# The first weight transfer of a convolution layer split into one contraction block each, the second half queued behind x's first block

## The chip, the cores and the metric

The kernel runs on one core of a Trainium2 chip. The metric is device microseconds (us) of one execution; each run gives one time, and the runs of a kernel are told by their median.

## The reference, cut to what matters

One layer of a convolution module over 1024 rows and 1024 channels, all in float32:

```
hn   = rms_norm(x) * norm_g                 # x: 1024 x 1024
a, b, gate = split(hn @ w_in, 3)            # w_in: 1024 x 3072
u    = a * sigmoid(b)
u    = depthwise causal conv of 31 taps over the rows + conv_b
u    = silu(layer_norm(u)) * silu(gate)
y    = x + u @ w_out                        # w_out: 1024 x 1024
```

## The kernel before, in words

Every float32 operand of a matmul is held as a high part, rounded to the matmul type (`w_hi`, `x_hi`), and a low part, the rest (`w_lo`, `x_lo`). One product is three matmuls: high by high, low weight by high x, high weight by low x. ScalarE (ACT) makes the high parts by a copy with rounding, VectorE (DVE) or GpSimd (POOL) the low parts by a subtraction.

The input projection is cut into 24 units, a unit being 128 output channels. A unit takes the contraction over 1024 channels in eight blocks of 128 (k = 0 to 7), for each half h of the rows (512 columns of a matmul). All of the kernel's matmuls stand in one order on TensorE (PE), written out by hand. What follows concerns its head:

- TensorE first does 11 warm-up matmuls on a tile of ones (L756; the float32 type makes 22 instructions of them), which need nothing but that tile.
- Then come the first two units ("b" and "a" of channel block 0) on half 1, interleaved (`project_raw(1)`, `raw_term`, L651): for each k the three terms of both units, so six matmuls a block and 48 in all. x isn't normalized yet; the factor 1/rms is put on afterwards. A matmul waits on the count `w_first_hi` or `w_first_lo` of converted weight pieces and on the count of converted x blocks.
- The same two units follow on half 0. After its block k = 4, TensorE spreads the inverse rms of half 1 over the partitions with two matmuls (`spread_rms(1)`, L622 and L624). L622 needs the four high diagonals that VectorE makes from the inverse rms (L1082), L624 the four low ones (L1085).
- All other units (`project`, L634) and, after them, the output products (L710) follow.

SyncE (SP) issues the loads, all on one DMA queue, in an order written out by hand. For half 1: weight piece 0, x blocks 0 and 1, piece 1, x blocks 2 and 3, piece 2, x blocks 4 and 5, piece 3, x blocks 6 and 7 (`load_first_weights` L522, `load_columns` L499). A weight piece holds two contraction blocks of both units, 256 KB, 2 KB per partition; an x block is 256 KB as well. The identity, half 0's x blocks and rows 4 to 7 of x (512 KB each, `load_rows`, L495) come next, mixed; row tile 7 is queued just ahead of x block 4 of half 0. The third unit's weights (L504) and the taps wait on SP until the pieces that cover k < 4 are converted (L534).

ScalarE converts in the same order: piece 0 (`split_first`, L784), x block 0 (`split_raw`, L778), x block 1, piece 1, and so on; then half 0's x blocks, with a sum of squares of a row tile (L772) behind each of the first four. VectorE follows it with the low parts (L1107 and L1100); on half 0 it makes diagonals 4 and 5 before x block 4's low part, and 6 and 7 before block 5's (`DIAGS_BEFORE`, L74). GpSimd makes the inverse rms of each row tile (L1408, L1411), and the low part of the third unit's weights (L1424) once all of x's low parts are there.

`FIRST_PIECES` (L96) and `PIECE_BEFORE` (L97) say how many pieces there are and ahead of which x block each one is loaded and converted.

Of the kernel before, what the change touches and what calls it, by code (L numbers as in the profile page):

```python
# [11 lines left out]
P = 128  # L12
HALF = 512
# [19 lines left out]
for n in range(14 - POOL_TAPS):  # L33
# [57 lines left out]
         for part in (("22", "12") if (b, q) == (5, 3) else ADDS[b])]  # L91
# [1 line left out]
EARLIER_ADD = {(b, part, q): max([n for b2, part2, q2 in POSTS if (part2, q2) == (part, min(q, 3))  # L93
                                  for n in [POST[b2, part2, q2]] if n < POST[b, part, q]], default=None)
               for b, part, q in POSTS}
FIRST_PIECES = 4  # L96
PIECE_BEFORE = {0: 0, 2: 1, 4: 2, 6: 3}  # L97
WARM_UPS = 11


def gated_conv_layer(nc, x, x_t, w_first, w_in, w_out, per_channel, identity, out):
    T, D = x.shape
    NT, KC = T // P, D // P
# [29 lines left out]
    with ctx:  # L133
        def sb(name, shape, dt=F32, into=ctx):
            return into.enter_context(nc.sbuf_tensor(name, shape, dt))

        def sem(name):
            return ctx.enter_context(nc.semaphore(name))
# [6 lines left out]
        raw = sb("raw", [P, 2, KC * P])  # L145
# [63 lines left out]
        rms_ready = sem("rms_ready")  # L209
        w2lo_half_ready = sem("w2lo_half_ready")  # L210
        norm_in = sem("norm_in")
        w_first_in = [sem(f"w_first_in{i}") for i in range(FIRST_PIECES)]
        w_first_hi = sem("w_first_hi")
        w_first_lo = sem("w_first_lo")
        xhi_raw = sem("xhi_raw")
# [156 lines left out]
        def bank(job):  # L372
            return mm[:, BANK[job], :]
# [23 lines left out]
        def col_order(h, k):  # L397

            return KC * (1 - h) + k
# [8 lines left out]

        def first_raw(i):

            return raw[:].rearrange("p m c -> p (m c)")[:, HALF * i:HALF * (i + 1)]

        def first_raw_units(i):

            return first_raw(i).rearrange("p (m c) -> p m c", m=2)

        def first_units(w, i):

            ks = KC // FIRST_PIECES
            return w[:, 0:2, ks * i:ks * (i + 1), :].rearrange("p m k n -> p m (k n)")  # L420

        def nth(kind, m):

# [35 lines left out]
        def terms(hi1, lo1, hi2, lo2):  # L459
            return ((hi1, hi2), (hi1, lo2), (lo1, hi2))  # L460

        def half(h):
            return slice(h * HALF, (h + 1) * HALF)
# [28 lines left out]
        def _(sp):  # L492
            def load_rows(t):

                sp.dma_start(sgate[:, t, :], x[t * P:(t + 1) * P, :]).then_inc(x_sq_in[t], 16)  # L495

            def load_columns(h, k):

                sp.dma_start(nat[:, k, half(h)], x_t[h, k]).then_inc(xt_in[h][k], 16)  # L499

            def load_weights(m):

                kind, j = UNITS[m]
                sp.dma_start(raw[:, m % 2, :], w_in[PART[kind], j]).then_inc(raw_in[m % 2], 16)  # L504
# [14 lines left out]

            def load_first_weights(i):  # L520

                sp.dma_start(first_raw(i), w_first[i]).then_inc(w_first_in[i], 16)  # L522

            for k in range(KC):
                if k in PIECE_BEFORE:
                    load_first_weights(PIECE_BEFORE[k])
                load_columns(1, k)
            sp.dma_start(ident[:], identity).then_inc(ident_in, 16)
            for k in range(KC):
                for t in ROWS_BEFORE.get(k, ()):  # L530
                    load_rows(t)
                load_columns(0, k)
                if k == 5:
                    sp.wait_ge(w_first_lo, FIRST_PIECES // 2)  # L534
                    load_weights(2)
                    sp.dma_start(chan[:, KC:], per_channel[:, KC:]).then_inc(chan_in, 16)
            for t in range(TPH):
                load_rows(t)
                if t == 2:
                    sp.wait_ge(w_first_lo, FIRST_PIECES)  # L540
                    load_weights(3)
            for m in range(4, NU):
                if m == 5:
# [71 lines left out]
        def _(pe):  # L615
# [22 lines left out]

            def raw_term(m, h, k, i):

                piece = k // (KC // FIRST_PIECES) + 1
                if i == 0:
                    if h == 1:
                        pe.wait_ge(w_first_hi, piece)
                    pe.wait_ge(xhi_raw, col_order(h, k) + 1)
                elif i == 1:
                    pe.wait_ge(xlo_raw, col_order(h, k) + 1)
                elif h == 1:
                    pe.wait_ge(w_first_lo, piece)
                w, xx = terms(w_hi, w_lo, x_hi, x_lo)[i]  # L650
                return nc.tensor.matmul(bank(("unit", m, h)), w[:, m, k, :], xx[:, k, half(h)],  # L651
                                        start=(k == 0 and i == 0), stop=(k == KC - 1 and i == 1))

            def project_raw(h):

                for k in range(KC):
                    for i in (0, 2, 1):
                        for m in range(2):
                            ins = raw_term(m, h, k, i)
                            if (k, i) == (KC - 1, 1):  # L660
                                ins.then_inc(unit_ready[UNITS[m][0]], 1)
                    if (h, k) == SPREAD_AT[1]:
                        spread_rms(1)
# [102 lines left out]
        def _(act):  # L766
# [8 lines left out]
            def split_raw(h, k):  # L775

                act.wait_ge(xt_in[h][k], 16)
                nc.scalar.activation(x_hi[:, k, half(h)], nat[:, k, half(h)], ACT.Copy,  # L778
                                     scale=norm_g[:, k:k + 1]).then_inc(xhi_raw, 1)

            def split_first(i):

                act.wait_ge(w_first_in[i], 16)
                nc.scalar.activation(first_units(w_hi, i), first_raw_units(i), ACT.Copy).then_inc(w_first_hi, 1)  # L784
# [169 lines left out]
            for k in range(KC):  # L954
                if k > 0 and k in PIECE_BEFORE:
                    split_first(PIECE_BEFORE[k])
                split_raw(1, k)
# [110 lines left out]
        def _(dve):  # L1068
# [28 lines left out]
            def split_raw(h, k):  # L1097

                dve.wait_ge(xhi_raw, col_order(h, k) + 1)
                nc.vector.scalar_tensor_tensor(x_lo[:, k, half(h)], nat[:, k, half(h)], norm_g[:, k:k + 1],  # L1100
                                               x_hi[:, k, half(h)].bitcast(F32), ALU.mult,
                                               ALU.subtract).then_inc(xlo_raw, 1)

            def split_first(i):

                dve.wait_ge(w_first_hi, i + 1)
                nc.vector.tensor_tensor(first_units(w_lo, i), first_raw_units(i), first_units(w_hi, i).bitcast(F32),  # L1107
                                        ALU.subtract).then_inc(w_first_lo, 1)
# [23 lines left out]
            def conv_in(m, h):  # L1132

                _, j = UNITS[m]
                dve.wait_ge(unit_ready["a"], arrival(j, h))
                if (j, h) in RAW_ORDER:
                    dve.wait_ge(sig_scaled, 3 * RAW_ORDER.index((j, h)) + 3)
                else:
                    dve.wait_ge(sig_ready, arrival(j, h) - len(RAW_ORDER))
                if j >= 4:  # L1140
                    if j - 4 in STEP_END:
                        dve.wait_ge(steps_done, STEP[j - 4, "sum", HT - 1])
                    else:
                        dve.wait_ge(prod_ready, PRODUCT_END[j - 4])
                nc.vector.tensor_tensor(u[:, j % 4, 0:2, PAD + h * Q:PAD + (h + 1) * Q],
                                        bank(("unit", m, h)).rearrange("p (s q) -> p s q", q=Q),
                                        sig[:, h, :].rearrange("p (s q) -> p s q", q=Q), ALU.mult).then_inc(u_ready, 1)
# [128 lines left out]
            for k in range(KC):  # L1276
                if k > 0 and k in PIECE_BEFORE:
                    split_first(PIECE_BEFORE[k])
                split_raw(1, k)
# [298 lines left out]
```

## Time and profile before

| | |
|---|---|
| median of 3 runs | 354.58 us (354.42 to 354.72) |
| the profiled execution | 354.64 us, of which 352.8 us are its span |
| TensorE busy | 348.5 us, 99% of the span |
| VectorE, GpSimd, ScalarE busy | 91%, 76%, 66% |
| DMA | 43.51 MB, mean 123 GB/s; 9 tenths or more of the 16 engines' time in nearly all of the first 28 us |

The span runs from the first instruction to the last; the profiled execution's time is 1.8 us more, work around the program. All times below are from the span's start. The busy shares say which engine has room left over the whole span, not what a stretch waits for; for that the chain of waits and the timeline of the stretch are read. TensorE's weight loads (PEld) run beside its matmuls (PE), and the ends of matmuls are modelled, so starts are read rather than ends.

### The profile page before, as it was taken

How to read it: one execution, taken by the hardware profiler on the slowest of the kernel's cores; microseconds unless marked ns; L12 is line 12 of the kernel's file. 1: busy time of each engine (PE TensorE's matmuls, PEld its weight loads, DVE VectorE, ACT ScalarE, POOL GpSimd, SP SyncE). 2: the span in 40 equal slices, each digit the busy share in tenths (PEclk: the TensorE clock that was granted, in tenths of full speed). 3: DMA queues.
4: the chain of work that ended last, by engine and by line, in shares of the span. 5: the costliest groups of instructions: out<-in, count | busy, mean ns of one | idle time of the engine just before them, and what ended most of it. 6: DMA issues, size and time to landing. Idle time of an engine off the chain costs nothing.

```text
span 352.8 us, 4758 instructions
## 1 busy us (share of the span) xinstructions
PE 348.5 (99%) x1564; PEld 289.6 (82%) x1564; DVE 322.4 (91%) x516; ACT 232.0 (66%) x334; POOL 267.0 (76%) x192
## 2 busy tenths in 40 slices
PE   8999999999999999999999999999999999999996
PEld 8888888888888888888888888888888888878785
DVE  5679799999999999989999998998599999999972
ACT  6889685667936870998669777975784872443400
POOL 0119999999999999789999999895596551359240
PEclk9999999999999999999999999999999999999999
DMA  8995111201410321404110410441643498047152
GB/s 265 411 412 212 39 59 59 88 34 61 118 61 16 88 78 59 119 2 119 59 60 3 119 59 15 107 119 61 215 143 120 130 394 313 0 151 224 45 208 90
DMA packets 30520, 43.51 MB, mean 123 GB/s; under 512 B 18336, under 2 KB 18848, under 8 KB 30496
## 3 DMA queue, kind: packets, MB, share of 16 engines
q1 hardware_dynamic: 30352, 43.21, 36.5%
q8 instruction: 12, 0.20, 0.2%
q14 instruction: 12, 0.10, 0.1%
q10 hardware_dynamic: 144, 0.00, 0.0%
HBM read 34.82 MB, written 4.19 MB: 111 GB/s over the span
## 4 chain that ended last, share of the span: by engine, by line
PE 92%; DVE 5%; issue 1%; ACT 0%; DVEq 0%; ACTq 0%
PE mm L634 68%; PE acc L710 9%; PE mm L651 6%; PE mm L710 6%; DVE sgate L1254 2%; DVE nat L1266 2%; DVE x_lo L1234 1%; PE acc L756 1%; PE acc L691 1%; PE acc L701 1%; PE acc L628 0%; ACT x_hi L948 0%; PE acc L622 0%; PE acc L624 0%; DVE ones L1069 0%
## 5 line engine op out<-in xcount | busy, mean ns | idle before, releaser
L634 PE MATMUL mm<-x_hi,w_hi 128*128 128x512 f32 x352 | 137.4, 390 | 0.0
L634 PE MATMUL mm<-x_hi,w_lo 128*128 128x512 f32 x352 | 137.0, 389 | 0.0
L634 PE MATMUL mm<-x_lo,w_hi 128*128 128x512 f32 x352 | 137.0, 389 | 0.0
L1178 DVE SCALAR_TENSOR_TENSOR acc<-u,chan,acc 128x512 f32<-128x512 f32 x157 | 110.5, 748 | 0.1
L1484 POOL TENSOR_TENSOR pconv<-pconv,prod 128x512 f32<-128x512 f32 x60 | 78.4, 1349 | 1.3 <-ACT prod L865 1.3
L634 PEld LDWEIGHTS mm<-x_hi,w_lo 128*128 128x128 f32 x352 | 66.1, 188 | 13.8
L634 PEld LDWEIGHTS mm<-x_lo,w_hi 128*128 128x128 f32 x352 | 66.1, 188 | 13.6
L634 PEld LDWEIGHTS mm<-x_hi,w_hi 128*128 128x128 f32 x352 | 66.1, 188 | 13.4
L1178 DVE SCALAR_TENSOR_TENSOR acc<-u,w_sum,acc 128x512 f32<-128x512 f32 x90 | 67.2, 747 | 2.5 <-ACT acc L847 2.3
L865 ACT ACTIVATE prod<-u,chan 128x512 f32<-128x512 f32 x69 | 47.9, 716 | 19.9 <-POOL pconv L1484 18.5
L1428 POOL TENSOR_TENSOR w_lo<-raw,w_hi 128x1024 fp32r<-128x1024 f32 (+1 forms) x21 | 50.3, 2395 | 8.7 <-ACT w_hi L814 8.6
L1484 POOL TENSOR_TENSOR pool_before<-pool_before,prod 128x512 f32<-128x512 f32 x37 | 49.3, 1331 | 1.1
L1444 POOL TENSOR_TENSOR wb_lo<-raw,wb_hi 128x1024 fp32r<-128x1024 f32 x6 | 14.5, 2408 | 16.2 <-DVE x_lo L1234 10.8
L865 ACT ACTIVATE prod<-u,w_sum 128x512 f32<-128x512 f32 x30 | 21.5, 716 | 7.8 <-POOL pool_before L1484 7.4
L948 ACT ACTIVATE x_hi<-sgate 128x512 fp32r<-128x512 f32 x28 | 15.9, 625 | 16.0 <-DVE sgate L1254 16.0
L710 PE MATMUL acc<-wb_hi,x_hi 128*128 128x512 f32 (+1 forms) x68 | 25.8, 379 | 0.0
L710 PE MATMUL acc<-wb_lo,x_hi 128*128 128x512 f32 (+1 forms) x68 | 25.6, 377 | 0.0
L710 PE MATMUL acc<-wb_hi,x_lo 128*128 128x512 f32 (+1 forms) x68 | 25.6, 377 | 0.0
L814 ACT ACTIVATE w_hi<-raw 128x1024 fp32r<-128x1024 f32 x22 | 23.1, 1048 | 1.3 <-PE mm L634 0.9
L891 ACT ACTIVATE sgate<-nat 128x1024 uint16<-128x1024 uint16 x14 | 14.0, 1050 | 11.5 <-POOL nat L1475 8.9
L1234 DVE TENSOR_TENSOR x_lo<-sgate,x_hi 128x512 fp32r<-128x512 f32 x28 | 20.8, 801 | 0.0
L904 ACT ACTIVATE rows<-sgate 128x1024 uint16<-128x1024 uint16 x14 | 18.2, 1368 | 3.5 <-DMA sgate<-sgate 2.1
(109 smaller groups left out, 527.6 us busy)
## 6 DMA issues: line engine op xcount, KB each, us to landing
raw<-w_in SPq DMA_DIRECT2D x22, 512.0 KB, 3.3
nat<-x_t SPq DMA_DIRECT2D x16, 256.0 KB, 5.4
sgate<-x SPq DMA_DIRECT2D x8, 512.0 KB, 10.2
raw<-w_out SPq DMA_DIRECT2D x8, 512.0 KB, 3.3
nat<-x SPq DMA_DIRECT2D x8, 512.0 KB, 7.7
y<-nat SPq DMA_DIRECT2D x15, 256.0 KB, 2.2
raw_late<-w_out SPq DMA_DIRECT2D x4, 512.0 KB, 4.3
sig<-w_out SPq DMA_DIRECT2D x4, 512.0 KB, 4.1
```

Of the source, the lines that this page charges most:

```text
L634: ins = nc.tensor.matmul(bank(("unit", m, h)), w[:, m % 3, k, :], xx[:, k, half(h)], start=(k == 0 and i == 0), stop=(k == KC - 1 and i == 2))
L651: return nc.tensor.matmul(bank(("unit", m, h)), w[:, m, k, :], xx[:, k, half(h)], start=(k == 0 and i == 0), stop=(k == KC - 1 and i == 1))
L710: ins = nc.tensor.matmul(product_bank(b, q), v[:, k0 + k, rows], w[:, k, piece_columns(b, q)], start=(k == 0 and i == 0 and continued(b, q ...
L814: nc.scalar.activation(w_hi[:, m % 3, :, :].rearrange("p k n -> p (k n)"), raw[:, m % 2, :], ACT.Copy).then_inc(whi_ready, 1)
L865: nc.scalar.activation(dst, chain_in(j, chain, k), ACT.Identity, scale=tap(j, chain, k), bias=bias(j, chain) if k == 0 else 0.0).then_inc( ...
L904: nc.scalar.activation(words_of_rows(side)[:, :, :, i], crossed()[:, NT * i:NT * (i + 1), :], ACT.Copy).then_inc(rows_joined, 1)
L948: nc.scalar.activation(v_pair(b, k)[0], v_raw(b, k), ACT.Copy).then_inc(vhi_ready, 1)
L1178: ins = nc.vector.scalar_tensor_tensor(dst, chain_in(j, chain, k), tap(j, chain, k), chain_bank(j, chain), ALU.mult, ALU.add)
L1234: nc.vector.tensor_tensor(lo, v_raw(b, k), hi.bitcast(F32), ALU.subtract).then_inc(vlo_ready, 1)
L1428: nc.gpsimd.tensor_tensor(w_lo[:, m % 3, ks, :].rearrange("p k n -> p (k n)"), raw[:, m % 2, ks.start * P:], w_hi[:, m % 3, ks, :].rearran ...
L1444: ins = nc.gpsimd.tensor_tensor(lo, source, hi.bitcast(F32), ALU.subtract)
L1484: ins = nc.gpsimd.tensor_tensor(pool_sum(chain), summand, prod[:, SLOTTED.index((j, chain, k)) % 4, :], ALU.add)
```

## The change

Piece 0, which held contraction blocks 0 and 1 of both units, becomes two pieces of one block each; the other three pieces stay. The first (128 KB) is still the first load; the second (128 KB) is loaded and converted behind x's first block and ahead of its second. Since a partition of a piece now has to be laid out block by block, the host stores the pieces with the block outermost (block, unit, column), and the conversions read and write three-dimensional patterns (unit, block, column), where they had runs of 256. The two new loads read 1 KB per partition. TensorE's counts, and SP's two waits, follow the new number of pieces (SP waits for 3 pieces where it waited for 2, and for 5 where it waited for 4); the warm-ups stay 11.

```diff
-FIRST_PIECES = 4
-PIECE_BEFORE = {0: 0, 2: 1, 4: 2, 6: 3}
+FIRST_PIECES = ((0, 1), (1, 2), (2, 4), (4, 6), (6, 8))
+PIECE_BEFORE = {ks[0]: i for i, ks in enumerate(FIRST_PIECES)}
 WARM_UPS = 11
...
-        w_first_in = [sem(f"w_first_in{i}") for i in range(FIRST_PIECES)]
+        w_first_in = [sem(f"w_first_in{i}") for i in range(len(FIRST_PIECES))]
...
         def first_raw(i):
 
-            return raw[:].rearrange("p m c -> p (m c)")[:, HALF * i:HALF * (i + 1)]
+            k0, k1 = FIRST_PIECES[i]
+            return raw[:].rearrange("p m c -> p (m c)")[:, 2 * P * k0:2 * P * k1]
 
         def first_raw_units(i):
 
-            return first_raw(i).rearrange("p (m c) -> p m c", m=2)
+            return first_raw(i).rearrange("p (k m n) -> p m k n", m=2, n=P)
 
         def first_units(w, i):
 
-            ks = KC // FIRST_PIECES
-            return w[:, 0:2, ks * i:ks * (i + 1), :].rearrange("p m k n -> p m (k n)")
+            k0, k1 = FIRST_PIECES[i]
+            return w[:, 0:2, k0:k1, :]
...
             def load_first_weights(i):
 
-                sp.dma_start(first_raw(i), w_first[i]).then_inc(w_first_in[i], 16)
+                k0, k1 = FIRST_PIECES[i]
+                start = 2 * P * (k0 % 2)
+                sp.dma_start(first_raw(i), w_first[k0 // 2, :, start:start + 2 * P * (k1 - k0)]).then_inc(w_first_in[i], 16)
...
                 if k == 5:
-                    sp.wait_ge(w_first_lo, FIRST_PIECES // 2)
+                    sp.wait_ge(w_first_lo, PIECE_BEFORE[KC // 2])
...
                 if t == 2:
-                    sp.wait_ge(w_first_lo, FIRST_PIECES)
+                    sp.wait_ge(w_first_lo, len(FIRST_PIECES))
...
             def raw_term(m, h, k, i):
 
-                piece = k // (KC // FIRST_PIECES) + 1
+                piece = sum(ks[0] <= k for ks in FIRST_PIECES)
...
-    w_first = w_in[[1, 0], 0].reshape(2, P, KC // 2, 2 * P).transpose(2, 1, 0, 3).reshape(KC // 2, P, HALF)
+    w_first = w_in[[1, 0], 0].reshape(2, P, KC // 2, 2, P).transpose(2, 1, 3, 0, 4).reshape(KC // 2, P, HALF)
```

## Rows read from the trace of the kernel before

**Rows 1.** The page: TensorE's busy time, and its granted clock in 40 slices.

```profile
PE 348.5 (99%) x1564; PEld 289.6 (82%) x1564; DVE 322.4 (91%) x516; ACT 232.0 (66%) x334; POOL 267.0 (76%) x192
...
PEclk9999999999999999999999999999999999999999
```

**Rows 2.** The chain of waits in order of time: start us, us, what; the first 25 us.

```profile
1.03 5.07 PE acc L756 x22
6.10 17.92 PE mm L651 x78
...
24.25 0.23 PE acc L624
```

**Rows 3.** All waits of TensorE in the whole span: total us, times, longest us.

```profile
PE acc L756 <- DVE ones L1069: 1.0, 1, 1.0
PE mm L710 <- DVE x_lo L1234: 0.5, 1, 0.5
```

**Rows 4.** Weight loads of warm-ups and first units: ns min/median/max, first and last start us.

```profile
L756 PEld LDWEIGHTS acc<-ones x22: 288/333/338, 1.0 to 5.5; 128*128 128x128 f32 x22
...
L651 PEld LDWEIGHTS mm<-x_hi,w_hi x32: 187/188/333, 5.7 to 27.0; 128*128 128x128 f32 x32
```

**Rows 5.** Timeline, 0 to 12 us: start us, us, instruction [idle before <-releaser].

```profile
0.72 0.39 SPq L522 DMA_DIRECT2D raw<-w_first  x1
...
1.17 0.89 SPq L499 DMA_DIRECT2D nat<-x_t  x2
...
3.36 0.63 ACT L784 ACTIVATE w_hi<-raw 128x512 fp32r<-128x512 f32 x1 [0.71 <-DMA raw<-w_first]
...
4.16 0.72 ACT L778 ACTIVATE x_hi<-nat,chan 128x512 fp32r<-128x512 f32 x1 [0.17 <-DMA nat<-x_t]
...
6.48 0.63 ACT L784 ACTIVATE w_hi<-raw 128x512 fp32r<-128x512 f32 x1 [0.73 <-DMA raw<-w_first]
...
7.54 0.61 PE L651 MATMUL mm<-x_hi,w_hi 128*128 128x512 f32 x2
...
8.90 0.61 PE L651 MATMUL mm<-x_hi,w_hi 128*128 128x512 f32 x2
```

**Rows 6.** Stretches: us, each engine's busy time, PEclk, DMA share, GB/s.

```profile
4.00:5.00 1.00, 1.00 (x6) 1.00 (x6) 0.70 (x2) 0.72 (x1) 0.00 (x0) 1.00 1.11 231
...
14.30:15.20 0.90, 0.90 (x5) 0.74 (x5) 0.00 (x0) 0.90 (x3) 0.16 (x1) 1.00 0.99 396
15.60:16.00 0.40, 0.40 (x4) 0.32 (x3) 0.40 (x1) 0.38 (x1) 0.28 (x1) 1.00 1.05 430
```

**Rows 7.** Timeline, 11 to 24.3 us: the way to L624.

```profile
11.22 0.91 SPq L499 DMA_DIRECT2D nat<-x_t  x2
...
21.12 1.34 ACT L778 ACTIVATE x_hi<-nat,chan 128x512 fp32r<-128x512 f32 x2 [0.53 <-DMA nat<-x_t]
...
21.88 0.75 DVE L1100 SCALAR_TENSOR_TENSOR x_lo<-nat,chan,x_hi 128x512 fp32r<-128x512 f32 x1 [0.66 <-ACT x_hi L778]
...
23.45 0.35 DVE L1085 SCALAR_TENSOR_TENSOR diags<-ident,rms,diags 128x128 fp32r<-128x128 f32 x1
...
23.86 0.19 PEld L624 LDWEIGHTS acc<-diags,ones_r 128*128 128x128 f32 x1
...
24.09 0.39 PE L624 MATMUL acc<-diags,ones_r 128*128 128x512 f32 x1
```

**Rows 8.** Timeline, 24 to 36 us: the next low parts that TensorE needs.

```profile
26.42 1.31 POOL L1424 TENSOR_TENSOR w_lo<-raw,w_hi 128x512 fp32r<-128x512 f32 x1 [4.79 <-DVE x_lo L1100]
...
32.19 1.22 DVE L1113 TENSOR_TENSOR w_lo<-raw,w_hi 128x1024 fp32r<-128x1024 f32 x1
```

**Rows 9.** Groups by line and shape: busy us, mean ns of one, idle before.

```profile
L814 ACT ACTIVATE w_hi<-raw 128x1024 fp32r<-128x1024 f32 x22 | 23.1, 1048 | 1.3 <-PE mm L634 0.9 <-DMA raw<-w_in 0.4
...
L784 ACT ACTIVATE w_hi<-raw 128x512 fp32r<-128x512 f32 x4 | 2.5, 630 | 1.4 <-DMA raw<-w_first 1.4
```

```profile
L1107 DVE TENSOR_TENSOR w_lo<-raw,w_hi 128x512 fp32r<-128x512 f32 x4 | 2.7, 687 | 3.2 <-ACT w_hi L784 3.2
```

## The prediction, made before the changed kernel ran

> **What bounds the kernel now.** I read the page first. TensorE is busy 348.5 of 352.8 us, and its granted clock shows no dip [rows 1]. So the question is where the missing 4.3 us lie, and whether this change touches one of them. The list of TensorE's waits has two entries: 1.0 us at the very start, for the tile of ones, and 0.5 us late, in the output products [rows 3]. No wait on a weight piece or on an x block stands in it. The other 2.8 us are no waits of TensorE: they lie behind its last matmul, where the last results are added and stored. The chain of waits says the same in order of time: 22 warm-ups from 1.03 us, then 78 matmuls of the first units in one piece of 17.92 us [rows 2], which is 0.230 us each. A warm-up takes (5.7 - 1.03) / 22 = 0.212 us from start to start, and the first real weight load starts at 5.7 [rows 4], exactly where the last warm-up leaves off.
>
> Then I asked when the first real operands were ready. ScalarE ends piece 0's high part at 3.36 + 0.63 = 3.99 us and x's first block at 4.16 + 0.72 = 4.88 us, having waited 0.71 us and 0.17 us on the two loads [rows 5]. That is 0.8 us before TensorE asks. The head of the kernel is bound by the warm-ups, not by the loads that the change rearranges.
>
> **The change, part by part.** *The first operands.* The first load is 128 KB instead of 256 KB. At the 396 GB/s of a stretch that moves pieces of this sort [rows 6], 128 KB are 0.33 us; piece 0 can be there 0.33 us sooner, and x's first block too, with 128 KB less ahead of it. The high part of x's block 0 would end near 4.88 - 0.33 = 4.55 us. It makes a slack of 0.8 us into one of 1.1 us and is worth nothing, because the 11 warm-ups still end at 5.7.
>
> *The next blocks.* TensorE asks for block 1 at 7.54 and for block 2 at 8.90 us [rows 5]. The conversion of block 1's weights now stands between x's blocks 0 and 1. Even done in a row from the old 4.16 us, x 0.72 + weights 0.42 (worked out next) + x 0.72 end at 6.02, 1.5 us early. For block 2, ScalarE starts the weights at 6.48, as soon as they have landed; with its 0.63 and x's 0.72 the operands are there at 7.83, 1.07 us early [rows 5]. The low parts follow the high ones, and TensorE uses them later too, by two and four matmuls. All hidden, and hidden as long as the loads come less than about 1 us later than now.
>
> *ScalarE and VectorE.* One more instruction on each. A copy of 1024 columns takes 1048 ns, one of 512 takes 630 [rows 9], so 256 columns cost 630 - 209 = 421 ns; two of them instead of one of 512 add 0.21 us on ScalarE. VectorE's subtraction of 512 takes 687 ns [rows 9]; taken with the same fixed part, two of 256 add about 0.2 us. Both engines wait on loads soon after (ScalarE 0.73 us before piece 1, and 0.53 us before half 0's block 4 [rows 5, 7]), so this is covered. Without that cover it would cost at most those 0.2 us once. The three-dimensional patterns of the conversions have no row here; I take nothing for them, and at worst they lengthen each of the ten conversions by the 0.2 us of a second instruction, against the same cover of over 1 us before each block is needed.
>
> *SP's queue.* It gets one more issue: 0.39 us for a weight piece, 0.89 / 2 = 0.45 us for an x block [rows 5]. Everything behind it, up to and past half 0's blocks, is issued some 0.4 us later. What matters is whether the DMA engines would notice. Half 0's block 4 is issued at 11.22 us and landed only just before 21.12 [rows 7]: there are 10 us of backlog. So an issue later by 0.4 us is hidden, except at the very start, where there is no backlog yet: the first small piece may be through before the next load has been taken up. Between 0 and 0.45 us of the engines' time can be lost there.
>
> *The transfers themselves.* The bytes are the same, but 128 rows of 2 KB become 256 rows of 1 KB. Row tiles with 4 KB rows move at 430 GB/s, x blocks with 2 KB rows at 396 [rows 6]. Per engine (a sixteenth) that is 152 ns for 4 KB in one packet and 2 x 83 = 166 ns in two: 14 ns per additional packet. Each engine gets 8 packets more, so about 0.11 us. This is an estimate from those rows, since no load with rows of 1 KB stands in the trace. "DMA: Bandwidth & Descriptors" of the Trainium skill (Why small descriptors are slow) puts a fixed overhead of about 3 cycles on every packet; with its 850 MHz that is an estimate of 8 x 3 / 0.85 = 28 ns, and the sum below would be nearly zero by it.
>
> *Where a later load would arrive first.* I looked for a place where TensorE has no slack against the DMA stream, and there is one. Half 0's block 4 lands just before 21.12 us, where ScalarE has been idle 0.53 us for it; VectorE, idle 0.66 us for ScalarE, starts its low part at 21.88, then makes the diagonals of row tiles 6 and 7 without a gap, and ends the last at 23.45 + 0.35 = 23.80 us. The weight load of L624, which needs it, starts at 23.86 [rows 7]. It could start at 24.09 - 0.19 = 23.90 at the latest without holding up its matmul. So the slack is 0.04 us, and each further 0.1 us that the stream is late at block 4 is 0.1 us of TensorE, which nothing behind gives back: TensorE stays without a gap up to the output products. It is paid once. The next places have more room: behind L624 come the 18 matmuls of blocks 5 to 7, so the third unit starts near 24.09 + 19 x 0.23 = 28.4 and needs L1424's result of 27.73 us, and the fourth starts 24 x 0.23 = 5.5 us later and needs L1113's of 33.41 [rows 8], 0.5 us of room or more each, and a wait at L624 moves their users back too.
>
> **The sum.** Stream later by 0.11 us (packets) and, at the start, by something between 0 and 0.45; I take 0.03 for it, since the first packets come slowly anyway and the nearest rows to this are those of the backlog. Less 0.04 of slack, TensorE waits 0.1 us at L624. Gains: none. On the profiled execution 354.64 + 0.10 = 354.74; it lies 0.06 above the median of its runs, so the median should be 354.58 + 0.10, about 354.7. The bounds of this term are 0 (all absorbed; below nothing it can't go, as TensorE has no gap there to close) and 0.45 + 0.11 - 0.04 = 0.52.
>
> **The rivals.** A difference of 0.2%, which is 0.71 us, is about what a measurement here can tell from none.
>
> *Nothing arrives at all.* The stream catches up, or the small packets are cheaper than I put them: 354.6. For it speaks the 10 us of backlog; against it only the missing slack of L624.
>
> *The warm-ups end sooner than in this trace.* They take 333 ns per weight load where the same load takes 188 ns later [rows 4]: TensorE runs them at the lower of its two clocks (1.2 GHz) to the last one, and the 188 ns come with the first units, although the granted clock reads full. If the rise to 2.4 GHz came amid the warm-ups, they would be over sooner, x's first block would set the start, and the change would bring its 0.33 us: 354.25. Against it: three runs within 0.3 us of each other. "TensorE: Matmul & The Clock Gate" of the Trainium skill (Part 1) warns that the number of slow matmuls at a start differs from run to run; no spread of that kind shows in the runs here. Even this rival stays within 0.2%.
>
> *Slower, at L624.* The mechanism is the one above with its price at the upper bound: the stream loses the full issue time because it starts from nothing, 0.45 + 0.11 - 0.04 = 0.52, so 355.1. It is slower by more than 0.2% from the point at which block 4 of half 0 is late by over 0.75 us. That needs more than the issue, for instance a hole like the one at 4 to 5 us, where the engines move 231 GB/s [rows 6] and lose 1 - 231 / 396 = 0.42 us of stream, to grow to twice its size: 0.52 + 0.42, 355.5. I see no reason that it should, but I don't know what makes it.
>
> *It doesn't do what it says.* The first weights may not be converted sooner, because the first load's time is start-up rather than bytes. That changes no time here; it would only show at the first L784.
>
> **How the numbers follow.** A small wait at L624: 0.52. Nothing at all: 0.22. Warm-ups sooner: 0.08. The full issue time at L624: 0.09. More than 0.75 us: 0.06. A gain of over 0.2% by something I don't see: 0.03. The likeliest gives 354.7. The range takes in the first two, the wait of 0.52 us with a little room for the medians' own spread, 354.3 to 355.2, and leaves out 0.17. Faster by over 0.2%: 0.03; within: 0.52 + 0.22 + 0.08 + 0.09 = 0.91; slower: 0.06.
>
> **What would show it right or wrong.** In the changed kernel: five L784, the first near 3.0 us instead of 3.36, x's first conversion near 3.8 instead of 4.16, and the first real weight load still at 5.7, straight behind the warm-ups. If that load is earlier, my reading of the head is wrong. The conversion of half 0's block 4 starts near 21.25; if it starts at 21.12 or sooner, the stream lost nothing. The last L1085 ends near 23.9, and the weight load of L624 follows it directly with a wait of 0.1 us on VectorE, a new entry among TensorE's waits. The forecast is wrong if TensorE waits anywhere in the first 10 us, or if the time moves by over 0.7 us either way.

## The result, and the profile after

Timed in turn with the kernel before, the changed kernel took 356.21 us (355.33 to 356.29, 6 runs), the kernel before 354.73 (354.42 to 355.24, 6 runs): ratio 1.0034, 95% interval 1.0024 to 1.0044. I had forecast 354.7, in a range up to 355.2. It is slower by more than 0.2%, the case to which I gave 0.06.

Two later series timed the same kernel again, with 11 runs each: 355.56 against 354.84, 1.0018 (1.0007 to 1.0028), and 355.73 against 354.93, 1.0022 (1.0013 to 1.0031). So the loss is real and repeats; its size is between 0.7 and 1.5 us by the medians, and the run that stands here in detail is at the upper end. The profiles of the two later series lose their time in other places; they are compared below.

The page of the changed kernel, with the busy time of each engine:

```profile
span 354.5 us, 4761 instructions
...
PE 349.1 (98%) x1564; PEld 289.4 (82%) x1564; DVE 322.6 (91%) x517; ACT 232.2 (65%) x335; POOL 267.0 (75%) x192
```

The span is 1.7 us longer, TensorE's busy time only 0.6 [rows 1]: TensorE stands idle about a microsecond more. Where, its list of waits says (total us, times, longest us):

```profile
PE acc L759 <- DVE ones L1072: 1.0, 1, 1.0
PE mm L654 <- ACT x_hi L781: 1.0, 1, 1.0
PE mm L713 <- DVE x_lo L1237: 0.5, 1, 0.5
```

The first and the third entry are those of [rows 3]; the second is new. The chain of waits in order of time shows the place (the line numbers of TensorE's matmuls are three higher than before):

```profile
12.56 10.33 DMA nat<-x_t
...
22.92 0.73 ACT x_hi L781
...
23.69 1.65 PE mm L654 x6
...
25.35 0.47 PE acc L625
25.82 0.33 PE acc L627
26.14 4.10 PE mm L654 x18
30.24 6.81 PE mm L637 x30
```

Before, this stretch was TensorE's alone [rows 2]. Now the chain goes through the load of half 0's block 4, which is issued at 12.56 us and converted from 22.92 (before: 11.22 and 21.12 [rows 7]). TensorE waits for it, then for the diagonals behind it: the two matmuls take 0.47 and 0.33 us of the chain, where 0.23 each is their work. The third unit starts at 30.24 us, against 24.47 + 4.08 = 28.55 before. That is 1.69 us, the whole difference of the spans (354.5 - 352.8); what follows took as long as before.

The timeline of the same stretch shows that every step waits on the one before it (last bracket: idle time before the instruction, and what ended it):

```profile
22.92 1.35 ACT L781 ACTIVATE x_hi<-nat,chan 128x512 fp32r<-128x512 f32 x2 [0.86 <-DMA nat<-x_t]
23.67 0.75 DVE L1103 SCALAR_TENSOR_TENSOR x_lo<-nat,chan,x_hi 128x512 fp32r<-128x512 f32 x1 [0.93 <-ACT x_hi L781]
23.69 0.30 PEld L654 LDWEIGHTS mm<-x_hi,w_hi 128*128 128x128 f32 x2 [1.44 <-ACT x_hi L781]
...
25.23 0.35 DVE L1088 SCALAR_TENSOR_TENSOR diags<-ident,rms,diags 128x128 fp32r<-128x128 f32 x1
```

Why block 4 is late is seen far ahead of it, in the stretches of the first 10 us (last two columns: DMA share, GB/s):

```profile
3.00:4.00 1.00, 1.00 (x7) 1.00 (x7) 0.34 (x1) 0.51 (x2) 0.00 (x0) 1.00 0.94 279
4.00:5.00 1.00, 1.00 (x6) 1.00 (x6) 0.34 (x2) 0.93 (x2) 0.00 (x0) 1.00 0.75 234
5.00:6.00 1.00, 1.00 (x7) 1.00 (x6) 0.82 (x2) 0.03 (x1) 0.00 (x0) 1.00 0.93 358
6.00:7.00 1.00, 1.00 (x5) 0.82 (x5) 0.28 (x1) 1.00 (x2) 0.00 (x0) 1.00 1.04 227
7.00:8.00 1.00, 1.00 (x6) 0.81 (x5) 1.00 (x2) 0.95 (x2) 0.00 (x0) 1.00 0.82 293
8.00:9.00 1.00, 1.00 (x6) 0.83 (x5) 0.79 (x2) 0.08 (x2) 0.00 (x0) 1.00 0.71 223
9.00:10.00 1.00, 1.00 (x6) 0.84 (x5) 0.31 (x1) 1.00 (x2) 0.00 (x0) 1.00 0.93 326
```

Before, the same seven stretches read 397, 231, 305, 385, 375, 387 and 397 GB/s, with one hole at 4 to 6 us; now they read 279, 234, 358, 227, 293, 223 and 326. That is 2477 against 1940 KB, 537 KB less, or 1.3 us at 400 GB/s. From 10 to 20 us the mean rates are alike (408 against 411 GB/s). SP's issues tell of it too:

```profile
5.94 1.46 SPq L500 DMA_DIRECT2D nat<-x_t  x2
7.44 0.65 SPq L531 DMA_DIRECT2D ident<-identity  x1
8.14 0.74 SPq L500 DMA_DIRECT2D nat<-x_t  x1
8.92 0.66 SPq L496 DMA_DIRECT2D sgate<-x  x1
```

An issue here takes 0.65 to 0.77 us where most take 0.43 to 0.45. (The kernel before has slow ones too: 0.65 us at 4.95, 0.54 and 0.55 us near 7.) Half 0's block 4 is so issued 1.34 us later than before, and not 0.4. Whether SP's slow issues make the holes or only feel them, the profile doesn't say.

The head itself went as forecast. The first conversion starts at 3.13 us (3.36 before), x's first block at 3.91 (4.16), and the first real weight load still at 5.68, straight behind the warm-ups:

```profile
3.13 0.42 ACT L787 ACTIVATE w_hi<-raw 128x256 fp32r<-128x256 f32 x1 [0.48 <-DMA raw<-w_first]
...
3.91 0.72 ACT L781 ACTIVATE x_hi<-nat,chan 128x512 fp32r<-128x512 f32 x1 [0.36 <-DMA nat<-x_t]
...
4.53 0.40 ACT L787 ACTIVATE w_hi<-raw 128x256 fp32r<-128x256 f32 x1
...
5.68 0.55 PEld L654 LDWEIGHTS mm<-x_hi,w_hi 128*128 128x128 f32 x2
...
5.97 0.72 ACT L781 ACTIVATE x_hi<-nat,chan 128x512 fp32r<-128x512 f32 x1 [1.04 <-DMA nat<-x_t]
```

But x's second block, the load right behind the second small piece, is already 0.94 us late (5.97 against 5.03 us), and ScalarE has waited 1.04 us for it.

The changed kernel was profiled three times, once in each series, and the three executions differ. (A load is landed when the count that ScalarE waits for is complete: start of the issue plus the time to landing, which is given to 0.1 us.)

| | before | changed, 1st | changed, 2nd | changed, 3rd |
|---|---|---|---|---|
| time of this execution, us | 354.64 | 356.29 | 355.12 | 356.46 |
| moved from 3 to 10 us, KB | 2477 | 1940 | 2239 | 2253 |
| half 1, weights of block 2 converted from, us | 6.48 | 6.60 | 7.19 | 8.11 |
| half 0, block 3 landed, us | 18.2 | 19.6 | 19.2 | 19.8 |
| half 0, block 4 landed, us | 21.1 | 22.9 | 21.0 | 21.7 |
| third unit starts, us | 28.55 | 30.24 | 28.84 | 29.41 |

All three have moved less in the first 10 us and have half 0's block 3 a microsecond or more late. But only the first has block 4 late by as much. The third loses its time far ahead of it, in the first 10 us, at the weights of half 1's block 2:

```profile
2.58 5.51 DMA raw<-w_first
...
8.11 0.63 ACT w_hi L787
...
9.60 15.20 PE mm L654 x66
```

TensorE starts block 2 at 9.60 us there, where it did at 8.90 [rows 5]. The second execution has 0.10 us of idle time at that place and TensorE is held at the two matmuls that need the diagonals, which take 0.45 and 0.32 us.

### The profile page after: what moved, and what is told of

It reads as the page before. It is cut to its first block, busy times and chain, and to the rows that moved or that the text cites. A ratio compares the mean times of both kernels' runs of the same rounds, so it can differ in the third digit from the quotient of the medians.

```text
span 354.5 us, 4761 instructions
## 1 busy us (share of the span) xinstructions
PE 349.1 (98%) x1564; PEld 289.4 (82%) x1564; DVE 322.6 (91%) x517; ACT 232.2 (65%) x335; POOL 267.0 (75%) x192
## 4 chain that ended last, share of the span: by engine, by line
PE 72%; DVE 14%; issue 4%; SPq 3%; DMA 3%; ACT 2%; POOL 1%; DVEq 0%; ACTq 0%; POOLq 0%
PE mm L637 63%; DVE x_lo L1237 3%; PE acc L713 3%; PE mm L713 3%; DMA nat<-x_t 3%; DVE sgate L1257 3%; DVE nat L1201 2%; DVE nat L1269 2%; DVE nat L1222 2%; SPq L500 2%; PE mm L654 2%; DVE sgate L1230 1%; POOL spare L1455 1%; ACT mm L937 1%; SPq L525 1%
## 5 line engine op out<-in xcount | busy, mean ns | idle before, releaser
L1487 POOL TENSOR_TENSOR pconv<-pconv,prod 128x512 f32<-128x512 f32 x60 | 76.6, 1296 | 1.3 <-ACT prod L868 1.3
L868 ACT ACTIVATE prod<-u,chan 128x512 f32<-128x512 f32 x69 | 47.8, 715 | 19.9 <-POOL pconv L1487 18.4
L1431 POOL TENSOR_TENSOR w_lo<-raw,w_hi 128x1024 fp32r<-128x1024 f32 (+1 forms) x21 | 49.4, 2354 | 8.6 <-ACT w_hi L817 8.6
L1487 POOL TENSOR_TENSOR pool_before<-pool_before,prod 128x512 f32<-128x512 f32 x37 | 47.9, 1295 | 1.1
L907 ACT ACTIVATE rows<-sgate 128x1024 uint16<-128x1024 uint16 x14 | 18.2, 1369 | 3.5 <-DMA sgate<-sgate 2.2
```

Of the source, the lines that this page charges most:

```text
L868: nc.scalar.activation(dst, chain_in(j, chain, k), ACT.Identity, scale=tap(j, chain, k), bias=bias(j, chain) if k == 0 else 0.0).then_inc( ...
L907: nc.scalar.activation(words_of_rows(side)[:, :, :, i], crossed()[:, NT * i:NT * (i + 1), :], ACT.Copy).then_inc(rows_joined, 1)
L1431: nc.gpsimd.tensor_tensor(w_lo[:, m % 3, ks, :].rearrange("p k n -> p (k n)"), raw[:, m % 2, ks.start * P:], w_hi[:, m % 3, ks, :].rearran ...
L1487: ins = nc.gpsimd.tensor_tensor(pool_sum(chain), summand, prod[:, SLOTTED.index((j, chain, k)) % 4, :], ALU.add)
```

## The experiments

Each was timed in turn with the kernel before, with 11 runs of its own and 32 or 33 of the kernel before. Theory A: the additional small load near the start leaves the DMA engines short. Theory B: the rows of 1 KB cost the time.

**1 KB rows alone.** Piece 0 remains one load:

```diff
...
+                if i == 0:
+                    source = source.rearrange("p c -> (p c)").rearrange("(m p c) -> p m c", m=2, p=P)
+                    into = into.rearrange("p (m c) -> p m c", m=2)
...
```

> The kernel before, with piece 0 still one load of 256 KB, but read in 256 rows of 1 KB. Theory A (the loss comes from the additional load near the start, whatever its rows): nothing, within 0.3 us of before, half 0's block 4 converted from 21.1 us on as before. Theory B (the rows of 1 KB are the cost): most of the 1.5 us, about 356.0, block 4 near 22.9.

Measured 355.05 against 354.86 us, 1.0007 (0.9998 to 1.0015). That is at most 0.5 us and not told from nothing. This alone doesn't part it from the changed kernel at its lower sizes (1.0018, from 1.0007); that B isn't the main cause follows together with the run further down that keeps the rows of 1 KB and loses nothing. (Its profiled execution, 356.08 us, was the slowest of the 11 and is no picture of the others: block 4 is converted from 22.64 us there, although 2453 KB were moved from 3 to 10 us.)

**An additional load with 2 KB rows.** Piece 0 in two loads of 64 partitions, converted as one:

```diff
...
+                if i == 0:
+                    sp.dma_start(first_raw(0)[0:P // 2], w_first[0, 0:P // 2]).then_inc(w_first_in[0], 16)
...
+                if k == 0:
+                    sp.dma_start(first_raw(0)[P // 2:P], w_first[0, P // 2:P]).then_inc(w_first_in[0], 16)
...
-                act.wait_ge(w_first_in[i], 16)
+                act.wait_ge(w_first_in[i], 32 if i == 0 else 16)
```

> The kernel before, with piece 0 in two loads of 64 partitions each, rows of 2 KB as before, the second behind x's first block; it is converted as one piece once both are there. Theory A: slower by 1 to 1.6 us, the DMA rates of 3 to 10 us low as in the changed kernel, block 4 of half 0 near 22.9. Theory B: within 0.3 us of before.

Measured 355.72 against 354.86, 1.0026 (1.0017 to 1.0035): as much as the change costs, without any row of 1 KB. In its profile TensorE waits 0.9 us, but at the head, for x's first block: ScalarE is behind piece 0's second half there (first real matmuls at 6.46 us in the chain instead of 6.10). So a part of this loss is the experiment's own. The stretch of 4 to 5 us shows 168 GB/s, and 2234 KB are moved from 3 to 10 us; block 4 is converted from 21.71 us, not near 22.9. (The profiled execution, 355.25 us, was the fastest of the 11.)

**A small load moved early, none added.** The kernel before, with the identity (64 KB) behind x's first block:

```diff
                 load_columns(1, k)
-            sp.dma_start(ident[:], identity).then_inc(ident_in, 16)
+                if k == 0:
+                    sp.dma_start(ident[:], identity).then_inc(ident_in, 16)
```

> The kernel before, with the identity's load (64 KB, SP) moved from behind half 1's blocks to behind x's first block; no load is added, none of the weights is touched. Theory A (a small load among SP's first ones leaves the engines short, since loads come to them one by one and not by bytes): slower by 0.7 to 1.6 us, rates of 3 to 10 us low. Theory B (the rows or the layout of the weights): no change, 354.9.

Measured 355.43 against 354.84, 1.0013 (1.0003 to 1.0024). Slower, with the weights left alone and the number of loads up to block 4 unchanged. It is less than A's lower figure of 0.7 us. The stream shows what A said: 2176 KB from 3 to 10 us, and block 3 landed at 19.1 us.

**A delay, and no load.** The kernel before, SP held behind x's first block:

```diff
+                if k == 0:
+                    sp.wait_ge(table_ready, 1)
```

> The kernel before, with SP made to wait behind x's first block until ScalarE's first small instruction is done (near 2.65 us), so that every later load is issued 1.0 us later and no load is added. If the stream is hurt by late issues near the start (it has no backlog yet): block 4 of half 0 later by 0.5 to 1.0 us, time 0.4 to 0.9 us over before. If only an additional load hurts it: no difference.

Measured 355.41 against 354.93, 1.0016 (1.0007 to 1.0025). Weight piece 1 is issued at 3.04 us instead of 2.10, and block 4 is converted from 21.57 instead of 21.12. Its chain shows where TensorE loses it: the 78 matmuls take 0.15 us more than in [rows 2], the two behind them 0.31 and 0.33 us instead of 0.23 each:

```profile
6.09 18.07 PE mm L653 x78
24.16 0.31 PE acc L624
24.47 0.33 PE acc L626
```

Later issues alone do cost time here. The changed kernel, timed in the same series, took 355.73 us, 1.0022 (1.0013 to 1.0031), with 0.5 us of delay at the same piece; the two intervals overlap, so 0.94 us of delay isn't shown to cost less than the change does. But the stream differs: 2407 KB from 3 to 10 us, and block 3 landed at 18.2 us, as in the kernel before, where the changed kernel has it 1.0 to 1.6 us late. Most of the delay was gone by then: SP issues block 4 only 0.40 us later than before. Why this kernel still loses 0.5 us is open.

**The second piece issued by ScalarE.** The changed kernel, its loads and their sizes untouched:

```diff
-                if k in PIECE_BEFORE:
+                if k in PIECE_BEFORE and k != 1:
...
+            act.dma_start(first_raw(1), w_first[0, :, 2 * P:4 * P]).then_inc(w_first_in[1], 16)
```

> The changed kernel, with the second small piece's load issued by ScalarE, right behind the gains, instead of SP; SP issues as many loads as before the change. Theory A in the form that SP's queue is what is fed too slowly: back to the time of before, 354.7, block 4 near 21.1. In the form that the engines take small loads badly wherever they are issued: still 1 us or more slower, 355.7 to 356.3. Theory B: as the changed kernel, 356.2.

Measured 354.53 against 354.86, 0.9993 (0.9984 to 1.0002): the loss is gone. This is the experiment that decides, so it was timed again in one series with the changed kernel.

> The changed kernel a third time, beside its variant with the second small piece on ScalarE. Slower than before by 0.2 to 0.35% (355.5 to 356.2), with rates below 350 GB/s in most of the stretches from 3 to 9 us.

> The same kernel with the second small piece issued by ScalarE. If it is SP's place among its first loads that costs: at the time of before or up to 0.1% under it, and apart from the changed kernel by more than both intervals. If the first run was chance: like the changed kernel.

The changed kernel took 355.73 us, 1.0022 (1.0013 to 1.0031), the variant 354.73, 0.9995 (0.9987 to 1.0004); the intervals lie apart. (The changed kernel's rates were low again, but below 350 GB/s in three of the six stretches from 3 to 9 us, not in most.) The variant's stretches show but a shallow hole:

```profile
3.00:4.00 1.00, 1.00 (x7) 1.00 (x7) 0.42 (x1) 0.45 (x2) 0.00 (x0) 1.00 0.86 292
4.00:5.00 1.00, 1.00 (x9) 1.00 (x9) 0.00 (x0) 0.55 (x1) 0.00 (x0) 1.00 1.04 397
5.00:6.00 1.00, 1.00 (x6) 0.77 (x6) 0.71 (x2) 1.00 (x3) 0.00 (x0) 1.00 0.86 313
6.00:7.00 1.00, 1.00 (x6) 0.79 (x5) 1.00 (x4) 0.61 (x2) 0.00 (x0) 1.00 1.01 383
7.00:8.00 1.00, 1.00 (x6) 0.82 (x5) 0.80 (x3) 0.92 (x2) 0.00 (x0) 1.00 1.05 397
8.00:9.00 1.00, 1.00 (x6) 0.84 (x5) 1.00 (x2) 1.00 (x2) 0.00 (x0) 1.00 1.05 406
```

Block 4 is converted from 21.12 us, as before. The bytes, the rows of 1 KB and the number of loads are the same as in the changed kernel. What differs is who issues the piece, and three things with it: SP's later loads are issued 0.47 us sooner again, the piece itself is issued at 1.16 us instead of 1.63, and it goes through a DMA queue of its own (q10 in the profile, SP's is q1). So an additional load costs where SP issues it among its first ones. Whether SP's relief or the second queue beside the first does the work isn't told apart: both profiles moved more from 3 to 10 us than the kernel before (2710 and 2598 KB against 2477), which SP's relief alone, back to the issues of before, doesn't explain.

**The identity issued by ScalarE.** The changed kernel, with that load off SP:

```diff
-            sp.dma_start(ident[:], identity).then_inc(ident_in, 16)
...
+            act.dma_start(ident[:], identity).then_inc(ident_in, 16)
```

> The changed kernel, with the identity's load (64 KB) issued by ScalarE at the start instead of by SP at 7.4 us. If it is the number of issues on SP up to block 4 that counts, back to 354.7 +-0.3. If it is the shape of the first four loads, no gain: 356.2, perhaps 0.2 less or more.

Measured 355.36 against 354.86, 1.0016 (1.0002 to 1.0029). It met neither forecast clearly: SP issues as many loads up to block 4 as before the change, yet a loss remains. So the number of issues up to block 4 isn't all that counts; that it is the start which counts is the likelier reading. (Its profile, 354.76 us, is of the fastest run and shows no loss.)

**The order of the small piece.** The changed kernel, both small pieces ahead of x's first block:

```diff
-                if k in PIECE_BEFORE:
+                if k in PIECE_BEFORE and k != 1:
                     load_first_weights(PIECE_BEFORE[k])
+                if k == 0:
+                    load_first_weights(1)
                 load_columns(1, k)
```

> The changed kernel, with the second small piece loaded ahead of x's first block instead of behind it. Theory A: the same number of loads, as slow as the changed kernel, 356 +-0.3. If it is the alternation of weights and x that costs: back to 354.9.

Measured 355.01 against 354.84, 1.0010 (0.9999 to 1.0022). Less than A said, and told neither from the kernel before nor from the changed one (1.0018, in the same series). Its stream is late all the same: 2261 KB from 3 to 10 us, block 3 landed at 19.1 us. Whether the position of the second piece matters stays open. The changed kernel in that series, for which I had expected 355.9 to 356.4 us and which took 355.56 with low rates:

> The changed kernel once more, beside the others of this call. If the DMA stream's low rates of 3 to 10 us belong to the change, they are there again and the time is 355.9 to 356.4. If they were one execution's accident, the rates are those of before and the time is near 354.9.

**The two matmuls behind block 5.** In the changed kernel:

```diff
-SPREAD_AT = {1: (0, 4), 0: (3, 0, 2)}
+SPREAD_AT = {1: (0, 5), 0: (3, 0, 2)}
```

> The changed kernel, with the two matmuls L622 and L624 (now L625, L627) behind block 5 of half 0 instead of block 4. Theory A says that TensorE waits first for block 4 itself (1.0 us in the changed kernel) and then for the diagonals (0.7 us more): the second part goes, 0.3 to 0.7 us faster than the changed kernel, 355.5 to 355.9. If TensorE's time was lost elsewhere, no difference from the changed kernel.

Measured 355.34, 1.0019 (1.0008 to 1.0029), against 355.56, 1.0018, for the changed kernel beside it: no difference. The expectation failed. It was built on the first profile of the changed kernel, and this execution, like the third one of the changed kernel, loses its time at the weights of half 1's block 2: TensorE starts that block at 9.32 us, where before it did at 6.10 + 12 x 0.23 = 8.86. The matmuls behind block 5 run at 0.23 us, but the third unit's 30 take 7.00 us where 6.81 is their work:

```profile
2.58 5.20 DMA raw<-w_first
...
9.32 16.61 PE mm L654 x72
25.93 0.23 PE acc L625
26.17 0.23 PE acc L627
26.40 2.72 PE mm L654 x12
29.12 7.00 PE mm L637 x30
```

The last diagonal ends at 24.48 us here, and TensorE would have come to the two matmuls at 9.32 + 66 x 0.23 = 24.5 in their old place: they would hardly have waited, so this profile can't show what moving them is worth. Three further steps behind the weights of block 2 (block 4, the diagonals, the third unit's low part) hang on the same late stream; which of them holds TensorE differs from execution to execution.

**Fewer warm-ups.** Three runs on the head: the kernel before with 9 warm-ups; with the two matmuls behind block 5 as well; and both on top of the piece on ScalarE.

```diff
-WARM_UPS = 11
+WARM_UPS = 9
```

> The kernel before, with 9 warm-ups instead of 11, the rest untouched. The prediction's reading: the warm-ups set the start (real matmuls 0.4 us sooner, at 5.25 or when x's first block is converted, 4.9), but L624 has no slack, so TensorE waits there for what it has won: same time as before, within 0.2 us. Rival (the head alone counts): faster by 0.4 us or more.

> The kernel before, with 9 warm-ups and the two matmuls that need the diagonals moved behind block 5 of half 0. The reading: L624 lets go of the gain, the next bound (block 4 itself, the third unit's low part) has some 0.5 us, so 0.3 to 0.5 us faster than before, 354.4. Rival: TensorE waits for x's blocks or the third unit instead, no gain.

> The changed kernel with its second small piece issued by ScalarE, 9 warm-ups, and the two matmuls behind block 5. If the stream keeps up as it did in the run with the piece on ScalarE, this is the best of all, 354.0 to 354.3. If the gain there was chance, as the kernel before or slower, 354.8.

Measured against 354.97: 355.11, 1.0000 (0.9990 to 1.0009); 355.22, 1.0000 (0.9989 to 1.0011); 354.84, 0.9997 (0.9987 to 1.0008). The first met its number, but not for the reason given. Its chain:

```profile
1.03 4.21 PE acc L756 x18
5.24 18.63 PE mm L651 x78
23.87 0.23 PE acc L622
24.10 0.23 PE acc L624
```

The warm-ups end 0.86 us sooner, and the 78 matmuls then take 0.71 us longer than in [rows 2]; the two matmuls don't wait. The weight loads show why: the first real one starts at 5.06 us, when x's first block is there, and they take 330 ns, those of the lower clock, up to the one at 6.52; from 6.90 on they take 188. (The granted clock reads full throughout, so only these durations show it.) In the kernel before the loads get short between those of 6.33 and 6.62 us. So TensorE's clock rose no sooner, and the units' first matmuls ran at 1.2 GHz in the warm-ups' place. The other two gained nothing either, though they were meant to.

**One load on ScalarE in the kernel before.** x's block 1 of half 1, twice:

```diff
-                load_columns(1, k)
+                if k != 1:
+                    load_columns(1, k)
...
+            act.dma_start(nat[:, 1, half(1)], x_t[1, 1]).then_inc(xt_in[1][1], 16)
```

> The kernel before, with only the load of x's block 1 (half 1) issued by ScalarE instead of SP. Theory A in the form that SP hands loads over too slowly at the start, in the kernel before as well: the low rate at 4 to 5 us goes, block 4 of half 0 up to 0.4 us sooner, time 0 to 0.3 us under before. If the loads' number counts wherever they are issued: no difference.

> The kernel before with x's block 1 of half 1 issued by ScalarE, again. If SP's issues are short at the start in the kernel before as well: 0 to 0.3 us under before. Else no difference.

Measured 354.83 against 354.97, 0.9992 (0.9984 to 1.0001), and 354.58 against 354.93, 0.9992 (0.9984 to 1.0001). Twice the same, and twice the interval just reaches 1: likely some 0.3 us faster, not shown. The hole of [rows 6] at 4 to 5 us is gone in both profiles (402 and 400 GB/s, where the kernel before has 231), and they moved 2717 and 2629 KB from 3 to 10 us against 2477.

## Why the prediction was wrong

*What bounds the kernel.* Right, for the time before. The warm-ups set the start, and the sooner weights and x brought nothing: first conversion sooner by 0.23 us (forecast 0.33), x's by 0.25, the first real weight load at the same 5.68 us. One rival was priced against this reading: were the warm-ups over sooner, I said, the change would bring 0.33 us. By my own account of L624, whose slack is 0.04 us, TensorE would have waited there for what it had won.

*ScalarE and VectorE.* Right. The two small conversions take 0.42 and 0.40 us (forecast 0.42), and neither engine delays TensorE by it.

*Where a later load arrives first.* Right for the first profiled execution, and not the whole of it. I said that half 0's block 4 and the diagonals behind it are where TensorE has no slack, that each further 0.1 us of lateness is 0.1 us of time, and that nothing gives it back. That a late third unit is not made up shows in these profiled executions:

| kernel | third unit starts, us | time, us | difference |
|---|---|---|---|
| before | 28.55 | 354.64 | 326.09 |
| changed | 30.24 | 356.29 | 326.05 |
| SP delayed | 28.90 | 355.13 | 326.23 |
| identity early | 29.45 | 355.60 | 326.15 |
| second piece on ScalarE, again | 28.43 | 354.50 | 326.07 |

A time 1.65 us longer goes with a third unit 1.69 us later. Of all 18 profiled executions 14 have a difference of 326.05 to 326.31 us. The others lost time later as well: in the third one of the changed kernel, at 356.46 us, the third unit starts at 29.41, a difference of 327.05, and two waits of 0.4 and 0.2 us stand behind 250 us that the kernel before doesn't have. I missed two things. TensorE waited for block 4 itself, before it waited for the diagonals. And it waited at half 1's block 2, which I called hidden "as long as the loads come less than about 1 us later than now": the weights were converted 1.63 us later in the third execution (8.11 against 6.48), so the condition was right and was not met. With it came the sign that I had named myself, a wait of TensorE in the first 10 us.

*SP's queue: the step that failed.* "So an issue later by 0.4 us is hidden, except at the very start", and there I allowed from 0 to 0.45 us of the engines' time and took 0.03, because "the nearest rows to this are those of the backlog". The term measured 1.0 to 1.6 us at half 0's block 3 in the three profiles of the changed kernel, and 1.8 us at block 4 in the first (21.12 to 22.92); 0.45 was not even its upper bound. The time lost was 0.7 to 1.5 us. Ten microseconds from issue to landing say how many loads stand in line; they don't say that the engines get them fast enough. The view that says so is the rate, stretch by stretch, and I had it: 231 GB/s at 4 to 5 us, 305 behind it, in the midst of full rates [rows 6]. I read this hole as an oddity that would have to "grow to twice its size" for no reason that I saw. It was the sign that the stream had no slack at the start. The rival that I priced for it (355.5, chance 0.06) was the right one.

*The transfers themselves.* 0.11 us for rows of 1 KB: the experiment gives 0.2 us with an interval from -0.1 to 0.5, which agrees both with this and with the 0.03 us by the Trainium skill's overhead ("DMA: Bandwidth & Descriptors", Why small descriptors are slow); the run can't tell them apart.

*What is shown and what is argued.* Shown: the loss comes with the additional load on SP and goes when ScalarE issues it; rows of 1 KB are not its main cause; later issues alone cost time too; the load leaves less moved from 3 to 10 us in all three profiles, and TensorE is reached at more than one place, half 1's block 2 or half 0's block 4. Argued: that SP's first loads come to the engines at a pace per load. That would explain the early identity and the two half loads. It doesn't say why the holes go on to 9 us, nor how the identity on ScalarE left part of the loss, and it isn't parted from the rival that a second queue moves more than one. In the first profile the 1.3 us in the rates of 3 to 10 us make up most of the 1.4 us at block 3. In the third they make 0.6 of 1.6 us; the engines had moved 6.5 MB when block 3 landed there, against 6.2 MB before, so a part of its lateness isn't supply and stays open.

## What to carry to other kernels

A backlog from issue to landing isn't proof that the DMA engines are fed: read GB/s in stretches of a microsecond over the first loads, and take a dip below the steady rate as a warning that there is no slack; here a load of 64 KB moved into it cost 0.6 us, and one of 128 KB added to it 0.7 to 1.5. Before splitting a load to start sooner, see whether the first consumer waits for it at all; here it had 0.8 us to spare, and the split could only cost. If a split is wanted, try issuing the additional load from another engine's queue, which took the loss away here. And profile a slow kernel more than once: three executions of this one lost their time in different places.

## What the runs showed that I had not expected

The landing of half 0's block 4 has a second part. In the kernel before, the DMA view of 19.0 to 19.9 us shows a fetch of instructions among the data:

```profile
q8 instruction: 1, 0.02, 6.1%
```

The 6.1% of 16 engines over 0.9 us are 0.88 us, and it is one packet, so on a single engine. The changed kernel's first profile has the same between 20.6 and 21.6 us (5.8% of 1 us, 0.93 us). No experiment moved the fetch on purpose, but it moved by itself, and the 18 profiles fall into two groups. In nine of them (the kernel before and the changed kernel's first among them) it begins 2.1 to 2.5 us before block 4 lands, and block 4 lands 2.9 to 3.5 us behind block 3. In the other nine it begins 1.0 us before block 4's landing or after it, and the distance is 1.8 to 2.0 us. Where it begins 1.0 us before, block 5 is the late one, 0.7 to 1.5 us behind block 4 instead of 0.5 to 0.7. The difference of about 1 us is about what the fetch holds its engine. That it is the fetch is an inference, not a test; but it accounts for what the table of three executions shows: in the second and the third the stream is 1.0 and 1.6 us late at block 3, and yet block 4 lands at 21.0 and 21.7 us, since the fetch misses it. And the slack of 0.04 us at L624, on which the prediction rests, holds for executions in which the fetch has already delayed block 4: in those of the kernel before with 9 warm-ups it hasn't, and block 4 lands at 20.0 and 20.5 us instead of 21.1.

The number of warm-ups made no difference to the time: 9 instead of 11 changed nothing within 0.1%, as the matmuls that took their place ran at 1.2 GHz. The moment at which the clock rises also moved. Of the 15 profiles with 11 warm-ups, five have them busy for 5.1 us, as before, and ten for 4.2 to 4.9, since the last ones ran at 2.4 GHz; in the runs with the piece on ScalarE, both times, they are over about 0.8 us sooner than in [rows 2]:

```profile
1.03 4.29 PE acc L759 x22
5.33 18.22 PE mm L654 x78
...
23.55 0.47 PE acc L625
24.02 0.33 PE acc L627
```

This is the second run with the piece on ScalarE. There TensorE is ahead of the stream and waits at the two matmuls instead, 0.47 and 0.33 us: the gain at the head goes where the prediction's account of L624, and not its rival, has it go, and the Trainium skill's warning that the number of slow matmuls at a start differs from run to run ("TensorE: Matmul & The Clock Gate", Part 1) holds here after all.
